# GpSimd splits each weight panel in two halves of 512 columns, and the products wait for the second half at their fifth tile

## The chip, the cores and the metric

One core of a Trainium2 chip. The time is that of one launch on the device in microseconds (us); the kernel before took 3286.77 us (median of three runs, 3283.34 to 3288.76).

## The reference, cut to what matters

Four transformer layers on 512 tokens of width 1024, all in float32, two of one kind and then two of another:

```python
for l in range(2):                       # first kind
    proj = rmsnorm(x) @ w_in             # 1024 -> 10 x 1024 (+16 gates)
    ya = diff_attention(...) @ w_out_a   # 8 heads, two softmax maps each
    yb = mlstm_chunkwise(...) @ w_out_b  # 8 heads
    x = x + (sigmoid(ga) * ya + sigmoid(gb) * yb) @ w_o
for l in range(2):                       # second kind
    proj = rmsnorm(x) @ w_in             # 1024 -> 8 x 1024
    merged = sigmoid(a) * (retention(...) @ p_ret) + sigmoid(b) * (stick_breaking(...) @ p_sb)
    x = x + merged @ w_out
    x = x + relu(rmsnorm(x) @ w_up) ** 2 @ w_down     # 1024 -> 4096 -> 1024
x = rmsnorm(x)
```

All the weights together are some 512 blocks of 1024x128, and nearly all the arithmetic is in the products with them.

## The kernel before, in words

Every float32 operand of a product is written as a sum of two numbers of TensorE's shorter float32 kind, `hi` and `lo`, and a product is three matrix products: hi with lo, lo with hi, hi with hi (`product`, lines 557 to 559). Weights come in **panels** of 128 rows by 1024 columns (512 KB), 512 of them in the whole kernel, through a ring of four slots:

- SyncE (SP) starts the DMA of panel n+4 into a slot of `raw` when TensorE has used panel n up (semaphore `used`, line 457).
- GpSimd (POOL) waits for the landing, then writes `w_hi` with one TENSOR_SCALAR (line 538) and, when that has finished (semaphore `w_step`), `w_lo = raw - w_hi` with one TENSOR_TENSOR (line 541), each over all 1024 columns, and raises the semaphore `split` by one. GpSimd does nothing else after the start.
- TensorE waits for `split` and uses the panel. In `gemm` (line 565) a panel is eight tiles of 128x128, and each tile takes three products over 512 tokens, 24 in all, into one of two accumulator banks. `gemm` is called for 404 of the panels. `first_panels` starts a layer with two panels while the norm of the last tokens is still being computed: it takes the early 256 tokens of both panels, then the late 256. `project` uses a panel as two blocks of 512 columns and adds into four banks of tokens; in the second of a layer's two projections (`last`) three panels are held to the end, so that the tokens finish one block after another.

The engines' programs are written out by hand, each in its own order, and meet at semaphores. Around the products ScalarE (ACT) and VectorE (DVE) take accumulators out and do the attention and the norms. VectorE's steps that matter here: `normalised` (line 1465) makes xn, the normalised tokens of one block, and `h_low` (line 1472) the low part of its transposed tiles; `rotate` (lines 1543 to 1549) turns queries and keys in place, and `split` (lines 1457 and 1458) writes the hi and lo part of an operand; `r_weights_low` (line 1779) writes sw_lo, the low part of the retention weights. In the first layer kind `rotate` and `split` end with k_lo, in the second with rk_lo; a_lo is the low part of a finished branch, which the first `gemm` of `merge` on the branch waits for.

The two lines that matter most:

```python
nc.gpsimd.tensor_scalar(m.w_hi[:, slot], m.raw[:, slot], 1.0, 0.0, ALU.mult, ALU.add)
nc.gpsimd.tensor_tensor(m.w_lo[:, slot], m.raw[:, slot], m.w_hi[:, slot].bitcast(F32), ALU.subtract)
```

Of the kernel before, what the change touches and what calls it, by code (L numbers as in the profile page):

```python
# [23 lines left out]
F32 = mybir.dt.float32  # L24
# [4 lines left out]
ALU = mybir.AluOpType  # L29
# [6 lines left out]
KT = D // P  # L36
# [379 lines left out]
def program(nc, t, out):  # L416

    ctx = ExitStack()
    with ctx:
        m = Memory(nc, ctx)  # L420
        rows = nc.dram_tensor("rows", (B_HEADS // 2, 2 * S), F32, kind="Internal").ap()
        s = {name: ctx.enter_context(nc.semaphore(name)) for name in SEMAPHORES}
# [105 lines left out]
        @block.gpsimd  # L528
        def _(pool):
            at = Place(pool)  # L530

            def split_panel():

                slot = at.slot(RING)

                pool.wait_ge(raw_in[slot], at.at("panel", RING, div=RING, times=16))
                pool.sem_inc(s["w_step"], 1)
                nc.gpsimd.tensor_scalar(m.w_hi[:, slot], m.raw[:, slot], 1.0, 0.0, ALU.mult,  # L538
                                        ALU.add).then_inc(s["w_step"], 1)
                pool.wait_ge(s["w_step"], at.at("panel", 1, times=2))  # L540
                nc.gpsimd.tensor_tensor(m.w_lo[:, slot], m.raw[:, slot], m.w_hi[:, slot].bitcast(F32),  # L541
                                        ALU.subtract).then_inc(s["split"], 1)
                at.add("panel")

            with at.loop((DEPTH * (PANELS_L1 + PANELS_L2)) // RING, panel=RING):
                for _ in range(RING):
                    split_panel()

        @block.tensor
        def _(pe):  # L550
            at = Place(pe)
# [3 lines left out]
            def product(dst, hi, lo, rhs_hi, rhs_lo, first, last, **more):  # L555

                nc.tensor.matmul(dst, hi, rhs_lo, start=first, stop=False, **more)  # L557
                nc.tensor.matmul(dst, lo, rhs_hi, start=False, stop=False, **more)  # L558
                return nc.tensor.matmul(dst, hi, rhs_hi, start=False, stop=last, **more)  # L559

            def gemm(x_hi, x_lo):

                slot = at.slot(RING)
                c = at.n.get("acc", 0) % 2
                pe.wait_ge(s["split"], at.at("panel", 1))
                pe.wait_ge(acc_free[c], at.at("acc", 2, div=2))
                for k in range(KT):
                    w = slice(k * P, k * P + P)
                    mm = product(acc[c][:], m.w_hi[:, slot, w], m.w_lo[:, slot, w], x_hi[:, k], x_lo[:, k],
                                 k == 0, k == KT - 1)  # L570
                mm.then_inc(s["used"], 1)
                at.add("panel")
                at.add("acc")

            def first_panels():

                slots = [(at.n.get("panel", 0) + i) % RING for i in range(2)]
                banks = [acc[(at.n.get("acc", 0) + i) % 2] for i in range(2)]

                def half(i, tok):  # L580
                    for k in range(KT):
                        w = slice(k * P, k * P + P)
                        mm = product(banks[i][:, tok], m.w_hi[:, slots[i], w], m.w_lo[:, slots[i], w],
                                     m.h_hi[:, k, tok], m.h_lo[:, k, tok], k == 0, k == KT - 1)
                    return mm

                early, late = slice(0, 2 * P), slice(2 * P, S)
                turn_block(2)
                pe.wait_ge(s["split"], at.at("panel", 1))
                pe.wait_ge(acc_free[at.n.get("acc", 0) % 2], at.at("acc", 2, div=2))  # L590
                pe.wait_ge(s["h_ready"], at.at("norm", times=KT) + TB)
                half(0, early)
                turn_block(3)
                pe.wait_ge(s["split"], at.at("panel", 2))
                pe.wait_ge(acc_free[(at.n.get("acc", 0) + 1) % 2], at.at("acc", 3, div=2))
                half(1, early)
                pe.wait_ge(s["h_ready"], at.at("norm", times=KT) + KT)
                at.add("norm")
                for i in range(2):
                    half(i, late).then_inc(s["used"], 1)  # L600
                at.add("panel", 2)
                at.add("acc", 2)

            def project(x_hi, x_lo, tiles, ready, before, last):

                count = tiles // 2
                held = HELD if last else 1

                def part(q, b):
                    slot, tok = (at.n.get("panel", 0) + q) % RING, slice(b * P, b * P + P)  # L610
                    for k in range(2):
                        w = slice(k * 512, k * 512 + 512)
                        kt = 2 * q + k
                        mm = product(xb[b][:], x_hi[:, kt, tok], x_lo[:, kt, tok], m.w_hi[:, slot, w],
                                     m.w_lo[:, slot, w], kt == 0, kt == tiles - 1)
                    return mm

                for q in range(count - held):
                    pe.wait_ge(s["split"], at.at("panel", q + 1))
                    pe.wait_ge(s[ready], before + (2 * q + 2))  # L620
                    for b in range(TB):
                        if q == 0:
                            pe.wait_ge(s["x_done"], at.at("xb", times=TB) + (TB + b + 1))
                        mm = part(q, b)
                    mm.then_inc(s["used"], 1)
                for b in range(TB):
                    for q in range(count - held, count):
                        if b == 0:
                            pe.wait_ge(s["split"], at.at("panel", q + 1))
                            pe.wait_ge(s[ready], before + (2 * q + 2))  # L630
                        mm = part(q, b)
                        if b == TB - 1:
                            mm.then_inc(s["used"], 1)
                    if b < TB - 1:
                        mm.then_inc(s["xb_done"], 1)
                    if last and b in (1, 2):
                        turn_block(b - 1)
                at.add("panel", count)
                at.add("xb")
# [5 lines left out]
            def turn_block(b):  # L645

                pe.wait_ge(s["xn_ready"], at.at("norm", times=TB) + (b + 1))
                if b == 1:
                    misc_bank()
                elif b > 1:  # L650
                    pe.wait_ge(s["h_ready"], at.at("norm", times=KT) + (1, 4)[b - 2])
                for j in range(2):
                    for k in range(TB):
                        o = (j * TB + k) * P
                        mm = nc.tensor.transpose(turned[b][j][:, k * P:k * P + P], m.xn[:, b, o:o + P], m.ident[:])  # L655
                    mm.then_inc(s["xT_done"], 1)
# [70 lines left out]
            def h_gemm():  # L727
                gemm(m.h_hi, m.h_lo)
# [123 lines left out]
            def merge():  # L852
                with at.loop(KT, panel=4, acc=4):
                    h_gemm()
                    pe.wait_ge(s["branch_a"], at.at("merge", 1, times=KT))
                    gemm(m.a_hi, m.a_lo)
                    h_gemm()
                    pe.wait_ge(s["branch_b"], at.at("merge", 1, times=KT))
                    gemm(m.b_hi, m.b_lo)
                at.add("merge")  # L860

            def project_merged():
                for c in range(2):
                    project(m.u_hi, m.u_lo, KT, "u_ready", at.at("merge", -1, times=KT) + 1, c == 1)
# [7 lines left out]
            with at.loop(DEPTH, panel=PANELS_L1, acc=PANELS_L1 - PANELS_D, xb=2, norm=1, layer=1, merge=1,  # L872
                         a=A_HEADS, pair=B_HEADS // 2, misc=PE_MISC_L1):
                first_panels()
                pe.wait_ge(s["masks_ready"], 5)
                group_sum(0, 0)
# [57 lines left out]
            with at.loop(DEPTH, panel=PANELS_L2, acc=PANELS_L2 - PANELS_D - 2 * PANELS_DOWN, xb=6, norm=2,  # L934
                         merge=1, r=R_HEADS, half=2, misc=PE_MISC_L2):

                def attention_turn(first):
                    if first:
                        first_panels()
                    else:  # L940
                        h_gemm()
                        h_gemm()
# [1108 lines left out]
```

## Time and profile before

| | |
|---|---|
| median of the runs | 3286.77 us (3283.34 to 3288.76) |
| the profiled execution | 3282.25 us, span 3280.5 us |
| mean granted clock of TensorE | 0.996 of full speed |
| TensorE products (PE) | 3218.6 us busy, 98%, 15796 instructions |
| VectorE (DVE) | 1433.1 us, 44%, 2205 instructions |
| ScalarE (ACT) | 829.9 us, 25%, 1813 instructions |
| GpSimd (POOL) | 1815.2 us, 55%, 1028 instructions |
| DMA | 298 MB, 91 GB/s in the mean |

The span runs from the first to the last instruction of the profiled execution. An engine counts as busy from the start to the end of an instruction, also while the instruction stands and waits for something inside the chip; the idle time before an instruction is put down to the engine or DMA that released it. Matrix products overlap in TensorE's pipeline, so their ends reach into the next one; the distance from start to start is what one costs. Views of the trace are the table of waits, the time line of an engine in a stretch, and sums by stretch.

### The profile page before, as it was taken

To read this page: it belongs to the slowest core of one execution; us is meant where nothing else is said; L and a number is where in the kernel's file an instruction comes from. 1 tells how busy PE (TensorE), PEld (TensorE's weight loads), DVE (VectorE), ACT (ScalarE), POOL (GpSimd) and SP (SyncE) were. 2 spreads that over 40 slices of the span, in tenths; PEclk is the share of its full clock that TensorE was granted. 3 is DMA by queue.
4 is the path that set the end of the run, shared out by engine and by line. 5 is a ranking of instruction groups with operands and counts; after the bars stand their busy time and mean duration, and the time that the engine had idled before them with its cause. 6 is when DMAs were issued, how large, how long until landed. Compare 5 with 4: busy or idle time off the path is not lost.

```text
span 3280.5 us, 47208 instructions
## 1 busy us (share of the span) xinstructions
PE 3218.6 (98%) x15796; PEld 2694.6 (82%) x15796; DVE 1433.1 (44%) x2205; ACT 829.9 (25%) x1813; POOL 1815.2 (55%) x1028
## 2 busy tenths in 40 slices
PE   7999999999999999999999999999999999999999
PEld 6887888887888888888888888888888888888887
DVE  7777652137776541256664113111366661131111
ACT  4554341025554420022221002111122220021021
POOL 4444556654545456655554666666644556666664
PEclk9999999999999999999999999999999999999999
DMA  3222222232222222322222222222322222222222
GB/s 119 90 86 75 94 79 96 96 103 75 90 84 88 80 89 96 102 90 87 87 80 77 96 99 94 96 96 96 107 81 81 78 79 91 97 97 98 98 98 97
DMA packets 89647, 298.31 MB, mean 91 GB/s; under 512 B 12592, under 2 KB 13488, under 8 KB 89552
## 3 DMA queue, kind: packets, MB, share of 16 engines
q1 hardware_dynamic: 74592, 271.61, 24.8%
q10 hardware_dynamic: 14960, 25.40, 2.5%
q8 instruction: 63, 1.03, 0.1%
q14 instruction: 32, 0.26, 0.0%
HBM read 282.23 MB, written 2.13 MB: 87 GB/s over the span
## 4 chain that ended last, share of the span: by engine, by line
PE 91%; DVE 5%; issue 1%; DMA 1%; ACT 1%; POOL 0%; ACTq 0%; DVEq 0%; SPq 0%; POOLq 0%
PE bank L557 28%; PE bank L559 28%; PE bank L558 28%; PE bank L660 1%; PE bank L772 1%; PE bank L693 1%; PE bank L717 1%; DVE xn L1465 1%; DVE sw_lo L1779 1%; PE bank L805 1%; PE bank L655 1%; PE bank L706 0%; PE bank L669 0%; PE bank L672 0%; DMA rrq<-rq 0%
## 5 line engine op out<-in xcount | busy, mean ns | idle before, releaser
L538 POOL TENSOR_SCALAR w_hi<-raw 128x1024 fp32r<-128x1024 f32 x512 | 559.9, 1093 | 1398.8 <-DMA raw<-in_w_in 944.7
L541 POOL TENSOR_TENSOR w_lo<-raw,w_hi 128x1024 fp32r<-128x1024 f32 x512 | 1255.8, 2453 | 42.7
L557 PE MATMUL bank<-h_lo,w_hi 128*128 128x512 f32 (+1 forms) x2912 | 1130.2, 388 | 3.7 <-POOL w_lo L541 2.9
L559 PE MATMUL bank<-h_hi,w_hi 128*128 128x512 f32 (+1 forms) x2912 | 1115.9, 383 | 0.0
L558 PE MATMUL bank<-h_hi,w_lo 128*128 128x512 f32 (+1 forms) x2912 | 1114.8, 383 | 0.0
L557 PEld LDWEIGHTS bank<-h_lo,w_hi 128*128 128x128 f32 x2912 | 549.2, 189 | 108.1 <-POOL w_lo L541 3.7
L559 PEld LDWEIGHTS bank<-h_hi,w_hi 128*128 128x128 f32 x2912 | 548.6, 188 | 108.7
L558 PEld LDWEIGHTS bank<-h_hi,w_lo 128*128 128x128 f32 x2912 | 549.3, 189 | 102.2
L1487 DVE TENSOR_TENSOR x<-x,bank 128x512 f32<-128x512 f32 x64 | 44.0, 687 | 392.2 <-PE bank L559 391.9
L557 PE MATMUL bank<-w_lo,up_hi 128*128 128x512 f32 x512 | 199.5, 390 | 0.0
L559 PE MATMUL bank<-w_hi,up_hi 128*128 128x512 f32 x512 | 199.2, 389 | 0.0
L558 PE MATMUL bank<-w_hi,up_lo 128*128 128x512 f32 x512 | 199.2, 389 | 0.0
L1687 DVE TENSOR_TENSOR sig_b<-bank,sig_b 128x512 f32<-128x512 f32 x32 | 22.1, 692 | 326.0 <-PE bank L559 326.0
L1422 ACT ACTIVATE m<-bank 128x512 f32<-128x512 f32 x64 | 38.4, 600 | 435.3 <-PE bank L559 432.3
L1457 DVE TENSOR_SCALAR up_hi<-mm 128x512 f32 x64 | 31.7, 495 | 264.9 <-ACT mm L1424 264.9
L1682 DVE TENSOR_TENSOR sig_a<-bank,sig_a 128x512 f32<-128x512 f32 x32 | 22.1, 692 | 225.7 <-PE bank L559 225.7
L559 PEld LDWEIGHTS bank<-w_hi,up_hi 128*128 128x128 f32 x512 | 96.1, 188 | 20.0
L557 PEld LDWEIGHTS bank<-w_lo,up_hi 128*128 128x128 f32 x512 | 96.1, 188 | 19.8
L558 PEld LDWEIGHTS bank<-w_hi,up_lo 128*128 128x128 f32 x512 | 96.1, 188 | 19.8
L557 PE MATMUL bank<-a_lo,w_hi 128*128 128x512 f32 x256 | 99.7, 390 | 4.4 <-DVE a_lo L1458 4.4
L1169 ACT ACTIVATE sig_b<-bank 128x512 f32<-128x512 f32 x32 | 19.2, 598 | 333.9 <-PE bank L559 333.9
L557 PE MATMUL bank<-w_lo,u_hi 128*128 128x512 f32 x256 | 100.3, 392 | 0.0
(285 smaller groups left out, 4440.7 us busy)
## 6 DMA issues: line engine op xcount, KB each, us to landing
raw<-in_w_in SPq DMA_DIRECT2D x288, 512.0 KB, 3.3
raw<-in_w_up SPq DMA_DIRECT2D x64, 512.0 KB, 3.2
raw<-in_w_down SPq DMA_DIRECT2D x64, 512.0 KB, 3.3
raw<-in_w_out_a SPq DMA_DIRECT2D x16, 512.0 KB, 3.2
raw<-in_w_out_b SPq DMA_DIRECT2D x16, 512.0 KB, 3.3
raw<-in_w_o SPq DMA_DIRECT2D x16, 512.0 KB, 3.3
raw<-in_p_ret SPq DMA_DIRECT2D x16, 512.0 KB, 3.2
raw<-in_p_sb SPq DMA_DIRECT2D x16, 512.0 KB, 3.3
```

What stands on the lines that cost most here:

```text
L538: nc.gpsimd.tensor_scalar(m.w_hi[:, slot], m.raw[:, slot], 1.0, 0.0, ALU.mult, ALU.add).then_inc(s["w_step"], 1)
L541: nc.gpsimd.tensor_tensor(m.w_lo[:, slot], m.raw[:, slot], m.w_hi[:, slot].bitcast(F32), ALU.subtract).then_inc(s["split"], 1)
L557: nc.tensor.matmul(dst, hi, rhs_lo, start=first, stop=False, **more)
L558: nc.tensor.matmul(dst, lo, rhs_hi, start=False, stop=False, **more)
L559: return nc.tensor.matmul(dst, hi, rhs_hi, start=False, stop=last, **more)
L655: mm = nc.tensor.transpose(turned[b][j][:, k * P:k * P + P], m.xn[:, b, o:o + P], m.ident[:])
L660: mm = nc.tensor.transpose(dst[:, b * P:b * P + P], src(b), m.ident[:])
L693: mm = nc.tensor.matmul(sq[k][qb], q[r, tok], key[r, keys], start=part == 0, stop=part == 2)
L717: mm = nc.tensor.matmul(pv[:, qb * P:qb * P + P], m.p1[:, o:o + P], m.v[:, sb], start=sb == 0, stop=sb == qb)
L772: mm = nc.tensor.matmul(m.bank[2 + qb // 2][:, o:o + B_DV + 1], m.e[a][:, w:w + P], m.va[a][:, sb, 0:B_DV + 1], start=sb == 0, stop=sb == qb)
L1422: own(activation(m.m[j % 2][:], acc[c][:], ACT.Relu))
L1487: tt(xs, xs, xb[b][:], ALU.add).then_inc(s["x_done"], 1)
```

## The change

GpSimd's two instructions become four: for each half of 512 columns a TENSOR_SCALAR and, after a wait, a TENSOR_TENSOR. `split` rises by two a panel, `w_step` by three. `gemm` waits for the first half before its first tile and for the second before its fifth. `first_panels` and `project` wait for both halves of a panel, with their counts doubled.

```diff
@@ split_panel
                 pool.sem_inc(s["w_step"], 1)
-                nc.gpsimd.tensor_scalar(m.w_hi[:, slot], m.raw[:, slot], 1.0, 0.0, ALU.mult,
-                                        ALU.add).then_inc(s["w_step"], 1)
-                pool.wait_ge(s["w_step"], at.at("panel", 1, times=2))
-                nc.gpsimd.tensor_tensor(m.w_lo[:, slot], m.raw[:, slot], m.w_hi[:, slot].bitcast(F32),
-                                        ALU.subtract).then_inc(s["split"], 1)
+                for half in range(2):
+                    w = slice(half * 512, half * 512 + 512)
+                    nc.gpsimd.tensor_scalar(m.w_hi[:, slot, w], m.raw[:, slot, w], 1.0, 0.0, ALU.mult,
+                                            ALU.add).then_inc(s["w_step"], 1)
+                    pool.wait_ge(s["w_step"], at.at("panel", times=3) + (half + 2))
+                    nc.gpsimd.tensor_tensor(m.w_lo[:, slot, w], m.raw[:, slot, w], m.w_hi[:, slot, w].bitcast(F32),
+                                            ALU.subtract).then_inc(s["split"], 1)
@@ gemm
-                pe.wait_ge(s["split"], at.at("panel", 1))
+                pe.wait_ge(s["split"], at.at("panel", times=2) + 1)
                 pe.wait_ge(acc_free[c], at.at("acc", 2, div=2))
                 for k in range(KT):
+                    if k == KT // 2:
+                        pe.wait_ge(s["split"], at.at("panel", times=2) + 2)
@@ first_panels
-                pe.wait_ge(s["split"], at.at("panel", 1))
+                pe.wait_ge(s["split"], at.at("panel", 1, times=2))
...
-                pe.wait_ge(s["split"], at.at("panel", 2))
+                pe.wait_ge(s["split"], at.at("panel", 2, times=2))
@@ project (two places)
-                    pe.wait_ge(s["split"], at.at("panel", q + 1))
+                    pe.wait_ge(s["split"], at.at("panel", q + 1, times=2))
```

## Rows read from the trace of the kernel before

**Rows 1.** The page: busy us, share, instructions of each engine

```profile
PE 3218.6 (98%) x15796; PEld 2694.6 (82%) x15796; DVE 1433.1 (44%) x2205; ACT 829.9 (25%) x1813; POOL 1815.2 (55%) x1028
```

**Rows 2.** TensorE's waits: who waited for whom, us, times, longest us

```profile
PE bank L557 <- DVE rk_lo L1458: 6.9, 2, 3.5
PE bank L693 <- DVE k_lo L1458: 5.4, 2, 3.0
...
PE bank L557 <- DVE sw_lo L1779: 5.3, 6, 1.0
PE bank L557 <- DVE a_lo L1458: 4.4, 2, 2.2
PE bank L557 <- POOL w_lo L541: 2.9, 3, 1.0
```

**Rows 3.** GpSimd's time line: start us, us, instruction [idle before it]

```profile
1441.67 2.71 POOL L541 TENSOR_TENSOR w_lo<-raw,w_hi 128x1024 fp32r<-128x1024 f32 x1
1444.35 1.50 POOL L538 TENSOR_SCALAR w_hi<-raw 128x1024 fp32r<-128x1024 f32 x1
```

**Rows 4.** VectorE's time line in the same stretch, ahead of rk_lo

```profile
1438.56 2.11 DVE L1543 TENSOR_TENSOR rq<-rq,cos 128x512 f32<-128x512 f32 x1 [10.90 <-DMA rrq<-rq]
...
1442.16 2.77 DVE L1545 TENSOR_TENSOR rq<-rq,rrq 128x512 f32<-128x512 f32 x1
...
1454.23 0.69 DVE L1458 TENSOR_TENSOR rk_lo<-rk,rk_hi 128x512 fp32r<-128x512 f32 x1
```

**Rows 5.** Sums around it: busy us (instructions) by engine, clock, DMA

```profile
1436.00:1466.00 30.00, 26.54 (x114) 22.10 (x113) 21.36 (x20) 4.29 (x9) 18.44 (x10) 0.89 0.25 81
```

**Rows 6.** VectorE's time line, first and last step ahead of k_lo

```profile
739.07 1.64 DVE L1543 TENSOR_TENSOR xq<-xq,cos 128x512 f32<-128x512 f32 x1 [5.60 <-DMA rot_q<-xq]
...
752.25 0.69 DVE L1458 TENSOR_TENSOR k_lo<-xk,k_hi 128x512 fp32r<-128x512 f32 x1
```

**Rows 7.** All engines' time line at a layer's start, around 2350

```profile
2348.47 1.05 POOL L538 TENSOR_SCALAR w_hi<-raw 128x1024 fp32r<-128x1024 f32 x1 [12.31 <-DMA raw<-in_w_in]
...
2349.55 1.28 DVE L1465 SCALAR_TENSOR_TENSOR xn<-x,sm,g_row 128x1024 f32<-128x1024 f32 x1 [1.35 <-ACT sm L1031]
2349.60 3.46 POOL L541 TENSOR_TENSOR w_lo<-raw,w_hi 128x1024 fp32r<-128x1024 f32 x1
...
2350.75 1.28 DVE L1472 TENSOR_TENSOR h_lo<-bank,h_hi 128x512 fp32r<-128x512 f32 x2
...
2353.12 0.39 PE L557 MATMUL bank<-h_lo,w_hi 128*128 128x256 f32 x1 [0.89 <-POOL w_lo L541]
```

**Rows 8.** The same at another layer's start, around 721

```profile
720.51 1.05 POOL L538 TENSOR_SCALAR w_hi<-raw 128x1024 fp32r<-128x1024 f32 x1 [12.12 <-DMA raw<-in_w_in]
...
721.79 3.32 DVE L1465 SCALAR_TENSOR_TENSOR xn<-x,sm,g_row 128x1024 f32<-128x1024 f32 x1 [1.35 <-ACT sm L1031]
```

**Rows 9.** All engines' time line before a_lo, around 1772

```profile
1771.85 1.05 POOL L538 TENSOR_SCALAR w_hi<-raw 128x1024 fp32r<-128x1024 f32 x1 [3.43 <-DMA raw<-in_p_sb]
...
1773.09 2.58 DVE L1457 TENSOR_SCALAR a_hi<-rg 128x512 f32 x1 [0.22 <-DVE rg L1808]
```

**Rows 10.** VectorE's time line around sw_lo

```profile
1547.21 3.83 DVE L1779 TENSOR_TENSOR sw_lo<-om,sw_hi 128x512 fp32r<-128x512 f32 x3 [0.41 <-ACT sw_hi L1252]
```

**Rows 11.** VectorE's time line at the start, the first three xn

```profile
14.03 5.75 DVE L1465 SCALAR_TENSOR_TENSOR xn<-x,sm,g_row 128x1024 f32<-128x1024 f32 x3
```

**Rows 12.** TensorE's time line at a panel's end and the next's start

```profile
564.70 0.39 PE L558 MATMUL bank<-b_hi,w_lo 128*128 128x512 f32 x1
564.93 0.39 PE L559 MATMUL bank<-b_hi,w_hi 128*128 128x512 f32 x1
565.16 0.39 PE L557 MATMUL bank<-h_lo,w_hi 128*128 128x512 f32 x1
```

**Rows 13.** All engines' time line, last panel of a projection

```profile
1974.54 2.40 POOL L541 TENSOR_TENSOR w_lo<-raw,w_hi 128x1024 fp32r<-128x1024 f32 x1
...
1977.49 0.39 PE L557 MATMUL bank<-w_lo,u_hi 128*128 128x512 f32 x1
```

More of the change, by code:

```diff
@@ L628, in project @@
                         if b == 0:
-                            pe.wait_ge(s["split"], at.at("panel", q + 1))
+                            pe.wait_ge(s["split"], at.at("panel", q + 1, times=2))
                             pe.wait_ge(s[ready], before + (2 * q + 2))
```

## The prediction

> **What bounds the kernel now.** Read the page first: TensorE is busy for 3218.6 of the 3280.5 us of the span, GpSimd (POOL) for 1815.2 [rows 1]. So GpSimd's splitting can cost time only through the 62 us in which TensorE idles, and through TensorE's clock. The table of who TensorE waited for names the places [rows 2]: it waits for the weight split itself in three places, 2.9 us in all, but for VectorE's results (rk_lo, k_lo, sw_lo, a_lo) over 20 us. The next view to open is therefore not GpSimd's but VectorE's time line ahead of these waits, beside GpSimd's.
>
> There the reader is to see one thing. VectorE's instructions on `rq`, 128x512, take 2.11 and 2.77 us, and one of the same kind and shape (`rk_lo`) takes 0.69 a few us later [rows 4]. The long one at 1442.16 lies beside a GpSimd TENSOR_TENSOR (2.71 from 1441.67), the short one does not [rows 3, 4]. One engine stands while the other runs, for the whole instruction, and the turn changes at each instruction's end: the VectorE product issued at 1442.16 ends at 1444.93, 0.55 after GpSimd's TENSOR_TENSOR (1444.38); GpSimd's next TENSOR_SCALAR then ends at 1445.85, 0.92 after that product [rows 3, 4]. VectorE instructions that read PSUM and one SBUF tile (h_lo) are not held: two take 1.28 together inside a GpSimd TENSOR_TENSOR [rows 7].
>
> **The change part by part.** *GpSimd's instructions.* Each of 512 panels gets four instructions of 512 columns for two of 1024. A whole TENSOR_SCALAR takes 1.05 alone and 0.92 behind a VectorE instruction; a TENSOR_TENSOR 2.40 alone and some 2.25 behind one (1441.67 + 2.71 = 1444.38, the VectorE instruction before the one at 1442.16 having ended about 1442.12) [rows 3, 4, 7, 13]. So some 0.14 of each is a fixed part that passes while it stands in the queue. No row shows a half. Its bounds are half of the whole (0.52 and 1.20) and the whole (1.05 and 2.40); I take half of the streaming part plus the fixed part: 0.60 and 1.25 alone, 0.46 and 1.10 behind a VectorE instruction, as 0.14 is what the nearest rows show. A panel then takes 0.60 + 0.08 + 1.25, twice, 3.9 instead of 3.5. In steady state that is hidden: panels follow each other every 5.4 us of products, and the ring is four deep.
>
> The Trainium skill ("GPSIMD Engine Reference", § 3.1, the reconciling table) tells against this: it charges every GpSimd instruction two software hops of dispatch, and gives 4497 ns for a two-input add of 2048 columns. With the 2.40 of this trace for 1024 that makes a fixed part of 0.30, an estimate from that page. By it the gain of 16 summed below would shrink to some 11, as each half that holds VectorE would cost some 0.1 more; page and trace differ, and the sum goes by the trace.
>
> *TensorE's waits.* `gemm` is called 404 times and waits once more, at its fifth tile. Queued behind that wait are the twelve remaining products, and behind them everything on TensorE. The trace has the like of it: at a panel's start there are two waits, and the first product follows the last of the panel before by 0.23, as inside a panel (0.23) [rows 12]. To the last digit that is at most 0.01, 4 us in all; I take 0. The split is ready long before in nearly every `gemm`, so the earlier half buys nothing there. `first_panels` and `project` still wait for whole panels.
>
> *Where GpSimd itself ends a wait: dearer.* In `first_panels` the second panel's TENSOR_SCALAR starts at 2348.47, VectorE's xn slips in at 2349.55, the TENSOR_TENSOR ends at 2353.06 and TensorE starts at 2353.12 [rows 7]. With halves: 2348.47 + 0.60 + 0.08 + 1.25 = 2350.40; xn now waits, and ends 1.08 later (its 1.28 less the part that overlaps the wait), 2351.48; + 0.46 + 0.08 + 1.25 = 2353.27. That is 0.2 to 0.3 later, at three places: +0.8. At the two layer starts where xn came just after the TENSOR_TENSOR it took 3.32 and ended at 725.11 [rows 8]; with halves it ends at 720.51 + 1.93 + 1.08 = 723.5, and the split 1.8 later at 725.3. TensorE's transposes (0.9) then end first and the split binds: 725.3 instead of 726.0, twice: -1.4.
>
> *Where VectorE ends a wait: cheaper.* Ahead of rk_lo stand ten dependent VectorE instructions from 1438.56 to 1454.92 [rows 4], held by seven GpSimd instructions. Taking turns with halves: eight of 0.55, two tensor_scalars of 0.28, the rest of a first half (0.6), then five halves of 1.10 and four of 0.46: 4.96 + 0.6 + 7.34 = 12.9, end at 1451.5. GpSimd's work is the same, but the chain is over before all of it has passed. TensorE waited 6.9 for rk_lo in two places [rows 2], so -6.8 of it goes; what is late next is TensorE's own product before. The same count for the second k_lo (eleven instructions, 739.07 to 752.94 [rows 6]; eight of 0.55, two of 0.28, the last 0.69, the same nine halves of 7.34 and 0.1 at the start) is 13.1 and gives -0.8, as there nearly all of GpSimd's work at hand still passes; the first k_lo counted so gives -0.5. For a_lo [rows 9]: the first a_hi waited for a whole TENSOR_TENSOR (2.58); with halves it waits from 1773.09 to 1773.78, and the later a_hi and a_lo pass one half each; a_lo comes 1.3 earlier, twice: -2.6. For sw_lo [rows 10] three instructions were held once, by one TENSOR_TENSOR; now they are held by the end of one half, a TENSOR_SCALAR half and another half, about as much: 0 to +0.1 at six places, +0.3.
>
> *The start.* The first three xn, issued at 14.03, take 5.75 and end at 19.78, where three of 1.28 would take 3.8 [rows 7, 11]: a TENSOR_TENSOR stands before them. Counted in turns (three xn of 1.08, two halves of 0.46 and 1.10 between them, and the chain before them 0.7 earlier, so that the first begins behind a half at 13.3) the third ends at 18.1: -1.7 for the first product.
>
> *The clock.* TensorE's granted clock is 0.89 over 1436 to 1466, where it idled 3.5 us for rk_lo [rows 2, 5]: 3.3 us of full clock missing, as 6.6 us at the lower of its levels, 1.2 GHz instead of 2.4. About half of that falls in the wait itself, where nothing runs, so 1.65 is lost. If the wait goes, that goes, in two places: -3.3; if the wait stays, nothing is won.
>
> The sum: -6.8 - 1.3 - 2.6 - 1.7 - 1.4 - 3.3 + 0.8 + 0.3 = -16.0 us. The profiled execution took 3282.25, so 3266; the median of the runs shown is 3286.77, 4.5 higher, and against it -16 makes 3271, which is what I forecast.
>
> **The rivals.** (a) *Hidden after all.* TensorE's waits for the split are only 2.9 us of 3280 [rows 2], and VectorE's gains may meet another wait at once: ScalarE's copies or the next transposed tile. For it: where VectorE works on without a break, GpSimd's total work is still paid, as for k_lo. Against it: before rk_lo TensorE had nothing else late. Then only the start, the layer starts and half of a_lo are left: about -4, 3283.
>
> (b) *Slower: the wait inside a panel drains TensorE.* Products follow each other without a gap only because the next is issued while one runs; if the sequencer stops at the fifth tile long enough to lose that, it costs up to one product's 0.23 [rows 12] in each of 404 calls, 93 us: 3364 after the gains. It decides from 0.04 a call (16 us, the whole gain). For it: the wait needs its own register arithmetic, in the middle of a run of products. Against it: the panel boundary has two such waits and shows no gap [rows 12].
>
> (c) *GpSimd's fixed part is large.* From 0.3 a half on, the last panel before each second projection is late: its split ends at 1976.94 for a product at 1977.49, 0.55 of slack [rows 13], and six places are like it. With 0.5 each split takes 1.0 longer: five layer starts +1.0 each, six projections +0.4 each, +7, and the VectorE gains fall to -8: about no change, 3286.
>
> **How the numbers follow.** Forecast, turns at every half: 0.6, between -8 and -22 (clock kept or not, fixed part up to 0.3), 3265 to 3279. (a): 0.2. (c): 0.12. (b) and the like: 0.08. A difference under 0.2%, 6.6 us, is what measurements of this kernel can't tell from none. Faster by more: the forecast and a little of (a), 0.62. Within: (a) and (c) for the most part, 0.29. Slower: (b) and the tail of (c), 0.09. The range, 3260 to 3288, takes in all waits of rows 2 gone at the lower end and no change at the upper; it leaves out (b).
>
> **What would show it.** Right: TENSOR_SCALAR halves near 0.6 and TENSOR_TENSOR halves near 1.25, no VectorE product of 512 columns above 2 us, no TensorE wait for rk_lo, a clock near 1.0 in the stretch around 1450, a_lo's wait near 1 us, and the three waits for w_lo longer by some 0.25. Wrong: halves of 0.9 and 1.6, a product pitch above 0.23 at the fifth tile, waits for w_lo inside `gemm`, or VectorE chains that end no earlier because GpSimd takes two turns to VectorE's one.

## The result and the profile after

The kernel after takes 3268.12 us (median of five runs, 3267.77 to 3269.92), the kernel before 3285.10 in the five runs beside them (3283.34 to 3288.76): a ratio of 0.9949, 95% interval 0.9938 to 0.9961, faster by 0.5%. Forecast were 3271.0, range 3260 to 3288. Between the profiled executions the span goes from 3280.5 to 3266.3 us, 14.2 less, and TensorE's mean granted clock from 0.996 to 0.998. The medians differ by 17.0: the profiled execution of the kernel before (3282.25) lies 2.9 under its median, that of the kernel after at its median.

The page of the kernel after, busy us of each engine, to be read against [rows 1]:

```profile
PE 3215.4 (98%) x15796; PEld 2690.8 (82%) x15796; DVE 1389.4 (43%) x2205; ACT 829.8 (25%) x1813; POOL 2082.5 (64%) x2052
```

GpSimd works 267 us more and the kernel is faster; VectorE's busy time, of which standing is a part, is 44 us less. GpSimd's groups of instructions (busy us, mean ns of one | idle us before them):

```profile
L543 POOL TENSOR_TENSOR w_lo<-raw,w_hi 128x512 fp32r<-128x512 f32 x1024 | 1395.6, 1363 | 85.4
L540 POOL TENSOR_SCALAR w_hi<-raw 128x512 fp32r<-128x512 f32 x1024 | 704.6, 688 | 1076.0 <-DMA raw<-in_w_in 733.9 <-DMA raw<-in_w_up 101.3 <-DMA raw<-in_w_down 94.8
```

Undisturbed halves (the medians) take 1.29 and 0.62 us. TensorE's waits of the kernel after, who waited for whom, us, times, longest, against [rows 2]:

```profile
PE bank L559 <- DVE sw_lo L1783: 7.4, 8, 1.1
...
PE bank L697 <- DVE k_lo L1462: 4.7, 2, 2.7
...
PE bank L559 <- POOL w_lo L543: 3.7, 5, 0.7
...
PE bank L559 <- DVE a_lo L1462: 2.2, 2, 1.1
...
PE bank L664 <- DVE hs L1660: 0.7, 3, 0.2
```

rk_lo has gone from the list, a_lo is halved; sw_lo has grown from 5.3 to 7.4 and hs is new. The stretch ahead of rk_lo, VectorE's time line of the kernel after (start us, us), to be laid beside [rows 4]:

```profile
1436.35 0.69 DVE L1547 TENSOR_TENSOR rq<-rq,cos 128x512 f32<-128x512 f32 x1 [11.71 <-DMA rrq<-rq]
1436.96 1.78 DVE L1548 TENSOR_TENSOR rrq<-rrq,sin 128x512 f32<-128x512 f32 x1
1438.78 0.98 DVE L1549 TENSOR_TENSOR rq<-rq,rrq 128x512 f32<-128x512 f32 x1
1439.80 1.40 DVE L1461 TENSOR_SCALAR rq_hi<-rq 128x512 fp32r<-128x512 f32 x1
1441.23 0.98 DVE L1462 TENSOR_TENSOR rq_lo<-rq,rq_hi 128x512 fp32r<-128x512 f32 x1
...
1447.43 1.66 DVE L1462 TENSOR_TENSOR rk_lo<-rk,rk_hi 128x512 fp32r<-128x512 f32 x1
```

and GpSimd's beside it:

```profile
1436.47 1.73 POOL L543 TENSOR_TENSOR w_lo<-raw,w_hi 128x512 fp32r<-128x512 f32 x1
1438.17 1.06 POOL L540 TENSOR_SCALAR w_hi<-raw 128x512 fp32r<-128x512 f32 x1
1439.31 1.60 POOL L543 TENSOR_TENSOR w_lo<-raw,w_hi 128x512 fp32r<-128x512 f32 x1
1440.88 0.80 POOL L540 TENSOR_SCALAR w_hi<-raw 128x512 fp32r<-128x512 f32 x1
```

Read the two as a zip, by the ends of the instructions: 1438.20 GpSimd's TENSOR_TENSOR, 1438.74 VectorE's rrq, 1439.23 GpSimd's TENSOR_SCALAR, 1439.76 VectorE's rq, 1440.91 GpSimd's next. Each starts its work when the other's instruction ends: about 0.55 for a VectorE product, 0.48 and 1.15 for a half. The chain takes 12.74 us (1436.35 to 1449.09) where it took 16.36.

The same stretch in sums, against [rows 5], and the stretch of the first k_lo in the kernel after and, last, before (us of each engine in the order PE, PEld, VectorE, ScalarE, GpSimd after the length; the clock is the last number but two):

```profile
1436.00:1466.00 30.00, 29.45 (x157) 24.81 (x157) 24.20 (x31) 7.82 (x14) 27.61 (x24) 1.00 0.24 77
...
45.00:60.00 15.00, 12.30 (x62) 8.71 (x61) 12.21 (x28) 8.42 (x21) 4.79 (x4) 0.89 0.01 2
```

```profile
45.00:60.00 15.00, 12.62 (x70) 8.28 (x69) 11.81 (x26) 7.27 (x16) 4.17 (x2) 1.00 0.01 2
```

TensorE no longer idles at rk_lo and its clock stays at 1.00; at the first k_lo it still waits, and the clock there is 0.89 (1.00 before).

### The profile page after: what moved, and what is told of

Read it like the earlier page. It is cut to its first block, busy times and chain, and to the rows that moved or that the text cites. A ratio compares the mean times of both kernels' runs of the same rounds, so it can differ in the third digit from the quotient of the medians.

```text
span 3266.3 us, 49148 instructions
## 1 busy us (share of the span) xinstructions
PE 3215.4 (98%) x15796; PEld 2690.8 (82%) x15796; DVE 1389.4 (43%) x2205; ACT 829.8 (25%) x1813; POOL 2082.5 (64%) x2052
## 3 DMA queue, kind: packets, MB, share of 16 engines
q8 instruction: 64, 1.05, 0.1%
## 4 chain that ended last, share of the span: by engine, by line
PE 92%; DVE 4%; issue 1%; DMA 1%; POOL 1%; ACT 1%; ACTq 0%; DVEq 0%; SPq 0%; POOLq 0%
PE bank L559 29%; PE bank L561 28%; PE bank L560 28%; PE bank L664 1%; PE bank L697 1%; PE bank L721 1%; PE bank L776 1%; DVE sw_lo L1783 1%; PE bank L809 1%; PE bank L710 0%; POOL w_lo L543 0%; PE bank L659 0%; PE bank L673 0%; PE bank L676 0%; POOL w_hi L540 0%
## 5 line engine op out<-in xcount | busy, mean ns | idle before, releaser
L543 POOL TENSOR_TENSOR w_lo<-raw,w_hi 128x512 fp32r<-128x512 f32 x1024 | 1395.6, 1363 | 85.4
L540 POOL TENSOR_SCALAR w_hi<-raw 128x512 fp32r<-128x512 f32 x1024 | 704.6, 688 | 1076.0 <-DMA raw<-in_w_in 733.9
L1461 DVE TENSOR_SCALAR up_hi<-mm 128x512 f32 x64 | 52.6, 822 | 247.1 <-ACT mm L1428 247.1
```

Source lines behind the costliest of these rows:

```text
L540: nc.gpsimd.tensor_scalar(m.w_hi[:, slot, w], m.raw[:, slot, w], 1.0, 0.0, ALU.mult, ALU.add).then_inc(s["w_step"], 1)
L543: nc.gpsimd.tensor_tensor(m.w_lo[:, slot, w], m.raw[:, slot, w], m.w_hi[:, slot, w].bitcast(F32), ALU.subtract).then_inc(s["split"], 1)
L1461: own(ts(hi, src, 1.0, None, ALU.mult))
```

## The experiments

Theory T: the gain is VectorE's, which gets its turn at the end of shorter GpSimd instructions, and TensorE's clock where a wait disappears; the wait at the fifth tile does nothing. Each run was timed beside the kernel before.

**Which half of the change.** The wait alone, taken away or put into the kernel before:

```diff
 e1: kernel after
-pe.wait_ge(s["split"], at.at("panel", times=2) + 1)
+pe.wait_ge(s["split"], at.at("panel", 1, times=2))
-                    if k == KT // 2:
-                        pe.wait_ge(s["split"], at.at("panel", times=2) + 2)
 e2: kernel before
+                    if k == KT // 2:
+                        pe.wait_ge(s["split"], at.at("panel", 1))
```

> The kernel after, but gemm waits for both halves of its panel before its first tile; no wait inside a panel. Theory T (the gain comes from VectorE getting its turn at the ends of the shorter GpSimd instructions; the wait at the fifth tile buys and costs nothing, as in the trace of after no gemm panel has its second half ready less than 2.9 us ahead of its first product): as the kernel after, 3268 within 2 us, the same waits of TensorE. Rival R1 (TensorE gains by starting on the first half of a panel): the gain goes, some 3280 to 3285. Rival R2 (the wait at the fifth tile costs TensorE something in each of 404 panels, 0.01 us or more, and hides part of the gain): 3264 or less.

> The kernel before, with whole GpSimd instructions, but gemm waits once more for its panel at the fifth tile. T: as the kernel before, 3285 within 2 us, each time 0.23 us from product to product at the fifth tile as elsewhere. R1: as before too, since there is no earlier half. R2: slower, by 4 us (0.01 a call) to 93 us (0.23 a call).

Measured: 3270.05 us, ratio 0.9950 (0.9936 to 0.9963), and 3282.60, ratio 0.9998 (0.9989 to 1.0007). Within these intervals, some 4 us for e1 and 3 for e2, the wait neither helps nor costs; R1 and R2 fall. In the kernel after, TensorE's time line across a fifth tile (its first product is the middle line):

```profile
568.52 0.39 PE L561 MATMUL bank<-h_hi,w_hi 128*128 128x512 f32 x1
568.75 0.39 PE L559 MATMUL bank<-h_lo,w_hi 128*128 128x512 f32 x1
568.98 0.39 PE L560 MATMUL bank<-h_hi,w_lo 128*128 128x512 f32 x1
```

0.23 as everywhere; over all 404 calls the distance into the fifth tile is 0.227 in the mean, 0.245 at most.

**Which of the two instructions.**

```diff
 e3: kernel before, TENSOR_SCALAR whole
+                for half in range(2):
+                    w = slice(half * 512, half * 512 + 512)
-                nc.gpsimd.tensor_tensor(m.w_lo[:, slot], ...)
+                    nc.gpsimd.tensor_tensor(m.w_lo[:, slot, w], ...).then_inc(s["split"], 1)
...                  TensorE waits for whole panels, with doubled counts
 e4: kernel before, TENSOR_TENSOR whole
+                for half in range(2):
-                nc.gpsimd.tensor_scalar(m.w_hi[:, slot], ...)
+                    nc.gpsimd.tensor_scalar(m.w_hi[:, slot, w], ...).then_inc(s["w_step"], 1)
...                  the count of w_step follows
```

> GpSimd's TENSOR_TENSOR (w_lo) in two halves, its TENSOR_SCALAR (w_hi) whole; TensorE waits for whole panels. T by turns (one GpSimd instruction passes for each VectorE instruction that uses two SBUF tiles, so what counts is the mean length of a turn: 1.6 us with two instructions a panel, 1.1 with three, 0.8 with four): about half to two thirds of the gain, rk_lo's chain some 2 us shorter of the 3.4 that TensorE waited, a_lo as in the kernel after: 3273 to 3279. Rival R4 (only the longest hold counts, the 2.4 us of the whole TENSOR_TENSOR): nearly the whole gain, 3268 to 3271. R1: no gain, 3285.

> GpSimd's TENSOR_SCALAR (w_hi) in two halves, its TENSOR_TENSOR (w_lo) whole; TensorE waits for whole panels. T by turns: rk_lo's chain gains as much as with the TENSOR_TENSOR in halves (three turns a panel again), but a_lo and the start, which stand behind one whole TENSOR_TENSOR, gain nothing: 3276 to 3282. R4 (only the longest hold counts): 3283 to 3286. R1: 3285.

Measured: 3278.16 (0.9980, 0.9971 to 0.9989) and 3283.55 (0.9996, 0.9987 to 1.0006). R4 falls with the first: with its longest hold gone the kernel has a third of the gain, not nearly all. T has the size of the first, though a_lo's wait is 4.0 us and not that of the kernel after, 2.2, as expected. The size of the second T has not: it is 1.5 us above T's range and inside R4's. TensorE's waits of e3:

```profile
PE bank L559 <- DVE a_lo L1460: 4.0, 2, 2.0
PE bank L559 <- DVE rk_lo L1460: 3.7, 2, 2.1
```

VectorE's time line of e4, ahead of rk_lo (chain 1442.11 to 1458.22):

```profile
1442.11 2.19 DVE L1545 TENSOR_TENSOR rq<-rq,cos 128x512 f32<-128x512 f32 x1 [11.97 <-DMA rrq<-rq]
1444.22 1.10 DVE L1546 TENSOR_TENSOR rrq<-rrq,sin 128x512 f32<-128x512 f32 x1
1445.35 0.98 DVE L1547 TENSOR_TENSOR rq<-rq,rrq 128x512 f32<-128x512 f32 x1
1446.37 2.50 DVE L1459 TENSOR_SCALAR rq_hi<-rq 128x512 fp32r<-128x512 f32 x1
...
1455.51 2.71 DVE L1460 TENSOR_TENSOR rk_lo<-rk,rk_hi 128x512 fp32r<-128x512 f32 x1
```

The turns explain e4's miss at rk_lo. Each of the ten steps stands behind one GpSimd instruction; which ones depends on where the chain begins. In e4 it begins in a TENSOR_TENSOR (rest 1.64) and then meets six TENSOR_SCALAR halves (0.46) and three whole TENSOR_TENSORs (2.25): 1.64 + 2.76 + 6.75 + 4.96 for VectorE's own work = 16.1, as measured; I had counted the mean of a panel, a third of each. e3's chain takes 15.0 us, the kernel after's 12.74. So each part alone shortens the chain by 0.3 (e4) or 1.4 (e3) of the 3.6, and TensorE still waits 3.0 and 3.6 us (e4) or 2.1 and 1.6 (e3) in the two places; only both take it past the 3.5 that TensorE waited. Taken from the starts of the same product in the traces, rk_lo with its clock is worth 0.8 us to e4, 6.0 to e3 and 11.8 to the kernel after. That is half of the 10 us by which 17 is more than 6.1 and 0.7; the start, the layer starts and a_lo also gain less alone, but one trace of each does not settle how the rest divides.

**Smaller turns, and the wait where it matters.**

```diff
 e5: kernel after, first_panels
-                pe.wait_ge(s["split"], at.at("panel", 2, times=2))
+                pe.wait_ge(s["split"], at.at("panel", 1, times=2) + 1)
-                half(1, early)
+                half(1, early, at.at("panel", 2, times=2))   # waited for at k == KT // 2
 e6: kernel after, GpSimd (e7: e5 and e6)
-                for half in range(2):
-                    w = slice(half * 512, half * 512 + 512)
+                for part in range(4):
+                    w = slice(part * 256, part * 256 + 256)
...
+                    if part % 2:
+                        lo.then_inc(s["split"], 1)
```

> The kernel after, and first_panels too waits for its second panel by halves: for the first half at the first tile, for the second half at the fifth. In the trace of after TensorE waits for the second panel's split at five layer starts (w_lo, 3.7 us in all), while xn's transposes are done some 0.8 us earlier. T: these waits go; TensorE starts 0.8 earlier and takes 1.4 us for four tiles of 256 tokens, by when the second half (0.8 later) is there: -3 to -4, 3264 to 3265.5. Rival (what ends the wait there is xn and its transposes as much as the split): 0 to -1, 3267 to 3268.

> The kernel after, with GpSimd's two instructions in quarters of 256 columns: eight turns a panel instead of four. From wholes and halves (1.05 and 0.62, 2.40 and 1.29) a quarter takes 0.40 or 0.74 alone and a panel 4.8 us instead of 4.0. T by turns: VectorE's holds are halved once more: k_lo, a_lo, sw_lo and hs come earlier, -6 to -11 in all; against it every split that ends a wait is 0.8 later, five layer starts +4, and the last panel of six projections, with 0.3 to 0.45 us to spare now, +0.4 each, +2.5. Sum 3261 to 3269, the waits for sw_lo and k_lo at half of 7.4 and 4.7, those for w_lo doubled. R4 (only holds of 2 us and more count, and these are gone): the losses alone, 3272 to 3276.

> Quarters and the layer starts by halves together. T: the gains of both, without the 4 us that quarters lose at the layer starts: 3256 to 3264. R4: 3268 to 3272.

Measured: e5 3266.41 (0.9943, 0.9929 to 0.9957). The waits for w_lo are gone and its five layer starts are 0.9 to 1.1 earlier, 5.3 in all, but only 1.7 shows, between T's range and the rival's: its second k_lo is waited for 0.5 longer with the clock lost again, and a wait for ScalarE's vTb near 1010 us is 3.5 instead of 1.9. That last wait is 1.9 in the trace of the kernel before and 3.3 to 3.9 in those of e1, e2, e3 and e4, also where GpSimd works as in the kernel before (e2); what sets it was not tried, so e5 alone is unresolved.

e6 3256.72 (0.9916, 0.9902 to 0.9929), 4 us below T's range; R4 falls again. A quarter takes 0.41 and 0.74 (medians). e6's waits, the longest:

```profile
PE bank L561 <- POOL w_lo L543: 12.8, 11, 2.2
...
PE bank L561 <- DVE a_lo L1464: 1.0, 2, 0.7
```

k_lo, sw_lo and hs are gone altogether, not halved; the split is now late in eleven places, as the forecast said. e7 makes TensorE wait by halves where that hurts: 3247.88 (0.9887, 0.9872 to 0.9902), w_lo 6.1 us, and 8 us below T's range, which had counted 4 us for the layer starts. Here, and not in gemm, the earlier half of a panel is worth 9 us.

**The six projections, the order, and six turns.**

```diff
 e11: e7, and project
-                    pe.wait_ge(s["split"], at.at("panel", q + 1, times=2))
+                    pe.wait_ge(s["split"], at.at("panel", q, times=2) + 1)
...
+                        if k and not b:
+                            pe.wait_ge(s["split"], at.at("panel", q + 1, times=2))
 e9: e11, in each half both TENSOR_SCALAR quarters, then both TENSOR_TENSOR quarters
 e10: e11, in each half one TENSOR_SCALAR of 512, then two TENSOR_TENSORs of 256
```

> Quarters, layer starts by halves, and now project too waits for its panels by halves. In the run of quarters with the layer starts by halves TensorE waits 0.36 to 0.99 us for the last panel's split at the six second projections (3.9 us in all). T: it starts on the first half, 2.4 us older, and needs the second 0.7 us later, when it is there: these waits go, -3 to -4, 3243.5 to 3245.5. Rival (the second half is waited for instead): 0 to -1, 3247 to 3248.

> As the kernel with layer starts and project by halves and quarters on GpSimd, but within each half both TENSOR_SCALAR quarters come before both TENSOR_TENSOR quarters, so that no TENSOR_TENSOR waits for the TENSOR_SCALAR just before it (0.08 us a time). T: the same number of turns, a panel 0.3 us shorter when alone: within 2 us of the other order, waits for w_lo a little shorter. Rival (the gap of 0.08 is what lets VectorE in; without it GpSimd takes two turns to VectorE's one): VectorE's holds are as with halves, +8 to +12.

> Layer starts and project by halves; GpSimd's TENSOR_SCALAR in halves and TENSOR_TENSOR in quarters: six turns a panel, mean 0.56 us behind a VectorE instruction (eight quarters: 0.43; four halves: 0.81), a panel alone some 4.2 us (4.8; 4.0). T by turns: chains of nine or ten turns (rk_lo, k_lo) 1.2 us longer than with quarters and 2.2 shorter than with halves, still off the path but for 0 to 0.5 us at k_lo; the split itself less late: within 4 us of quarters, 3242 to 3250. Rival (holds of up to 0.6 us, a whole instruction of 0.7, count as much as those of 1.1): near the halves with the layer starts, 3258 or more.

Measured: e11 3242.32 (0.9873, 0.9856 to 0.9889), e9 3244.58 (0.9884, 0.9867 to 0.9900), e10 3244.56 (0.9878, 0.9861 to 0.9894). Each is nearer to T than to its rival, and e10 is in T's range; e11 is 1.2 us below it (the six waits that went were 3.2 us in e7's trace, not 3.9), and e9 is 2.3 above e11 where T said 2. Which of the three is best the intervals don't tell. e11 beats both kernels, the kernel before by 42 us. In e9 VectorE still has a turn after each GpSimd instruction, and the chain ahead of rk_lo takes 9.1 us (8.8 in e11): the gap of 0.08 is not what lets it in. What TensorE still waits for in e11:

```profile
PE bank L671 <- DVE angles L1846: 11.2, 1, 11.2
...
PE bank L671 <- ACTq L1037: 4.8, 2, 2.5
PE bank L666 <- DVE xn L1476: 4.6, 2, 2.5
...
PE bank L561 <- POOL w_lo L543: 2.2, 5, 0.5
```

**The whole price of GpSimd's work.**

```diff
 e8: kernel after; the first four panels split whole
-                    w = slice(half * 512, half * 512 + 512)
+                    w = slice(half * 512, half * 512 + n)   # n = 16 after the first four
...
-                    mm = product(acc[c][:], m.w_hi[:, slot, w], m.w_lo[:, slot, w], ...
+                    mm = product(acc[c][:], m.w_hi[:, slot, w], m.w_hi[:, slot, w], ...   # so wherever panels are used
```

> The kernel after, with GpSimd splitting only 16 columns of each half after the first four panels (the products take w_hi of these four panels throughout, and w_hi in the place of w_lo): the same loads, products and waits, but next to no GpSimd work, so that VectorE is never held. It shows what GpSimd's work costs by holding VectorE and by being late itself. T: the waits for rk_lo, k_lo, a_lo, sw_lo, hs and w_lo all but vanish (some 19 us in after), with the clock lost behind k_lo: 3245 to 3254; the VectorE products of 512 columns all at 0.69 us. Rival R3 (TensorE's remaining waits for VectorE are VectorE's own chains, not holds): 3262 to 3266, only the waits for w_lo gone.

Measured: 3229.34 (0.9832, 0.9818 to 0.9845), clock 1.000, 16 us below T's range. VectorE's time line of e8, the same chain:

```profile
1412.59 0.69 DVE L1549 TENSOR_TENSOR rq<-rq,cos 128x512 f32<-128x512 f32 x1 [10.60 <-DMA rrq<-rq]
1413.19 0.71 DVE L1550 TENSOR_TENSOR rrq<-rrq,sin 128x512 f32<-128x512 f32 x1
...
1418.26 0.69 DVE L1464 TENSOR_TENSOR rk_lo<-rk,rk_hi 128x512 fp32r<-128x512 f32 x1
```

With next to no GpSimd work it takes 6.4 us for 12.7. R3 falls: the waits were holds. I had left out that two waits for ScalarE's vTb copies, 2.5 us each in e7 with the clock behind them, also go. GpSimd's work, by holding VectorE and by being late itself, thus cost the kernel before 56 us; the change got 17 of them, e11 42. e8 also multiplies other numbers, w_hi in the place of w_lo; at rk_lo, where e7 waits no more either, both come earlier than the kernel before by the same 6.5 and 5.3 us, so there the numbers show no time of their own.

## Why the prediction was right

The same product can be timed in both traces; the difference of the starts, taken ahead of and behind each place where it is steady, gives each term (us, one profiled execution of each kernel):

| term | forecast | measured |
|---|---|---|
| start, to the first product | -1.7 | -1.35 |
| first k_lo, with the clock | -0.5 | +1.85 |
| second k_lo, with the clock | -0.8 | -2.5 |
| rk_lo, two places, with the clock | -10.1 | -11.8 |
| a_lo, two | -2.6 | -2.2 |
| two layer starts (xn, then w_lo) | -1.4 | -1.4 |
| three layer starts (w_lo) | +0.8 | -0.1 |
| sw_lo (forecast six places, measured eight) | +0.3 | +2.6 |
| hs, five places | none | +1.8 |
| the rest (o_sb, vTb, last transposes) | none | -1.1 |
| sum | -16.0 | -14.2 |

That the sums lie so near is in part luck: the terms that came out dearer than forecast make +7.2 us, those that came out cheaper -5.4. Single terms also move from one execution to the next: taken for e2, whose GpSimd and VectorE instructions are those of the kernel before, the same difference is -1.35 at the second k_lo, +1.5 at the vTb near 1010 us and -0.6 at o_sb.

*rk_lo and the clock.* The mechanism is the one forecast and so is the chain: 12.9 counted, 12.74 measured. The product behind rk_lo came 3.6 us earlier in both places; 6 us on it was 6.4 in the first, and in all the two places gain 6.5 and 5.3. "About half of that falls in the wait itself" was too much. The kernel before, behind its two waits for rk_lo, in sums as above:

```profile
1455.06:1461.10 6.04, 6.04 (x20) 5.46 (x21) 3.20 (x7) 1.35 (x3) 3.40 (x2) 0.50 0.00 0
...
2382.30:2386.10 3.80, 3.79 (x15) 3.57 (x16) 1.26 (x3) 0.00 (x0) 3.40 (x2) 0.55 0.00 0
```

The products run at half clock for 6.04 us in the first place and at 0.55 for 3.80 in the second, 3.0 and 1.7 us lost behind the waits, where I took 1.65 each. At the second k_lo I counted no clock at all: its wait goes from 3.0 to 2.0 us, near the 0.8 forecast, and the clock behind it (0.89 over 750 to 765 us before, 1.00 after) makes the other 1.5. e2 keeps the clock there with a wait of 3.2, so these 1.5 are not shown to be the change's.

*The halves.* 0.62 and 1.29 against 0.60 and 1.25. With the wholes (1.05, 2.40) they make a fixed part of 0.19 and 0.18, and in the queue behind a VectorE instruction most of it passes unseen (half 0.48 and 1.15, whole 0.92 and 2.25). The fixed part estimated from the Trainium skill ("GPSIMD Engine Reference", § 3.1), 0.30, is more than the 0.18 measured here, and the trace's price was the one to sum by. Rival (c) is out with it: in the kernel after the six projections do not wait for the split, though 0.27 to 0.45 us are all that is left.

*Rival (a)* held at one place, the first k_lo, *rival (b)* nowhere: e2 puts the price of the wait at nothing within its interval.

*The mis-sized terms.* "About as much: 0 to +0.1 at six places" for sw_lo is the step that failed. At six of its eight places the three instructions take 3.8 to 3.9 us before and 3.95 to 4.13 after, and TensorE feels 0.1 to 0.3 of it. The other two, the first head of each layer, are not in the forecast, as TensorE did not wait there; they cost 0.8 and 0.7. VectorE and GpSimd around the first of them, in the kernel before and then in the kernel after:

```profile
1461.75 1.63 DVE L1779 TENSOR_TENSOR sw_lo<-om,sw_hi 128x512 fp32r<-128x512 f32 x3 [0.41 <-ACT sw_hi L1252]
...
1456.47 2.36 POOL L541 TENSOR_TENSOR w_lo<-raw,w_hi 128x1024 fp32r<-128x1024 f32 x1
1469.71 1.05 POOL L538 TENSOR_SCALAR w_hi<-raw 128x1024 fp32r<-128x1024 f32 x1 [10.88 <-DMA raw<-in_w_in]
```

```profile
1454.38 3.51 DVE L1783 TENSOR_TENSOR sw_lo<-om,sw_hi 128x512 fp32r<-128x512 f32 x3 [0.41 <-ACT sw_hi L1256]
...
1453.60 1.29 POOL L543 TENSOR_TENSOR w_lo<-raw,w_hi 128x512 fp32r<-128x512 f32 x1
1454.94 0.99 POOL L540 TENSOR_SCALAR w_hi<-raw 128x512 fp32r<-128x512 f32 x1
1456.02 1.60 POOL L543 TENSOR_TENSOR w_lo<-raw,w_hi 128x512 fp32r<-128x512 f32 x1
```

Before, GpSimd had split all that had landed by 1458.83 and then stood idle for 10.9 us, all the time that sw_lo took. After, it works without a break from the chain ahead of rk_lo to the end of sw_lo. The prediction says itself that this chain is over "before all of it has passed"; what is left stands beside the next chain, and that was not followed. Both places and the traces of e1 and e5 read alike; no run tries it alone. The third instruction, 128x256, was held nowhere before, at the six other places because the panel's one TENSOR_TENSOR had ended; now there is another half to stand behind (busy us, mean ns | idle us before them, before and then after):

```profile
L1779 DVE TENSOR_TENSOR sw_lo<-om,sw_hi 128x256 fp32r<-128x256 f32 x8 | 3.3, 413 | 0.0
```

```profile
L1783 DVE TENSOR_TENSOR sw_lo<-om,sw_hi 128x256 fp32r<-128x256 f32 x8 | 11.3, 1410 | 0.0
```

The rule behind the holds stands in the Trainium skill ("SBUF — State Buffer", "Who interferes with whom"): a VectorE instruction with two SBUF inputs contends with a GpSimd instruction that reads SBUF, and what they share is an exclusive lock. The trace agrees, 0.41 against 1.41 us for the same instruction; a short chain then pays for every boundary that it newly meets.

*hs and the first k_lo.* hs pays in another way: it stands behind the end of a panel's split, which is 0.4 later for the fixed parts (390.37 against 389.94 at the first). At the first k_lo VectorE's q_lo and the xk product after the rotation, 0.69 each before, newly stand behind halves and take 1.66 and 1.55. So k_lo comes only 1.0 earlier where TensorE comes 1.3 earlier, the wait grows from 2.4 to 2.7, and the clock falls to 0.89, as it does there in e1 and e5, which makes the other 1.5. I counted that chain by the pattern of the second k_lo instead of reading its own time line. Quarters take the waits for sw_lo, hs and k_lo away.

The three layer starts came out even, because with halves xn is late there (TensorE waits 0.4 to 0.5 for it) and the split ends no later for it.

## What to carry to other kernels

Where one engine's long instructions hold another, cut them until the chain that they hold is shorter than what it must beat; half of the way earned little here (6.1 or 0.7 of 17.0 us), as TensorE went on waiting. What a wait costs in TensorE's clock has to be read place by place: the clock was lost behind a wait of 2.1 us (e3, first rk_lo) and kept behind one of 3.2 (e2, second k_lo). Count a held chain in turns from where it begins, not by means; look for short chains that now slip past and will not, and follow the work that a shorter chain leaves over to the chain behind it. An earlier half is worth something only where the split is what TensorE waits for: at layer starts and projections here, not in the 404 calls that were changed.

## What the runs showed that I had not expected

- Halves of both instructions earn far more than the sum of either alone: -17.0 against -6.1 and -0.7 us.
- With quarters VectorE's busy time falls to 1260 us and GpSimd's rises to 2539, 78% of the span; the kernel is still faster by 28 us than before.
- The ten steps ahead of the first rk_lo take 6.4, 8.8, 12.7, 15.0, 16.1 or 16.4 us (e8, e11, after, e3, e4, before) with the same VectorE instructions, by GpSimd's alone.
- With the wait at rk_lo gone, sw_lo of each layer's first head, which TensorE had not waited for, takes 1.9 and 1.7 us longer.
